# A hybrid decoder layer on one core: the input projection by Strassen's seven products

## What is computed

```
h = rms_norm(x, norm_pre) * (1 + scale(c)) + shift(c)       # scale, shift, gate = silu(c) @ ada_w + ada_b
u = h @ w_in                                                # 1024 x 3720
q, k, v, f_logit, z_rwkv, p_pool, g = split(u)              # 512, 512, 512, 8, 896, 256, 1024 columns
y = concat[forgetting attention(rms_norm(q), rms_norm(k), v, f_logit),
           RWKV-7(z_rwkv), multi-window pooling(p_pool)] * silu(g)
x + gate(c) * rms_norm(y @ w_out, norm_post)
```

## Time and profile before

| | us |
|---|---|
| median of three runs (3635.56 to 3656.0) | 3651.18 |
| span of the profiled execution | 3646.8 |
| prepare, up to the projection's first instruction | 99.7 |
| projection, main part (first f matmul to last g matmul) | 112.5 to 1434.0 |
| recurrence, attention, output | 1439 to 3647 |

### The profile page before, as it was taken

One profiled execution on the slowest core, in us unless ns is written; L12 is line 12 of the kernel. 1 busy time (PEld: TensorE's weight loads), 2 busy tenths in 40 slices (PEclk: granted clock), 3 DMA queues, 4 the chain that ended last, 5 costly groups with the idle time before them and its releaser, 6 DMA issues. The chain is left out here.

```text
span 3646.8 us, 79839 instructions
## 1 busy us (share of the span) xinstructions
PE 3460.6 (95%) x26405; PEld 2109.1 (58%) x26405; DVE 2248.2 (62%) x3692; ACT 1867.6 (51%) x3525; POOL 1613.4 (44%) x2028
## 2 busy tenths in 40 slices
PE   8999999999999997699999599999999999979998
PEld 8444444444444443588888366666666666645444
DVE  7614152433424242688775499889988989964554
ACT  3322232232223233577775477777777777753333
POOL 0113030202112031245553389988889889962222
PEclk9999999999999998699988699999999999989999
DMA  8111212111111112222221221120220211214555
GB/s 331 53 50 67 71 48 65 54 62 54 66 53 65 58 64 77 54 76 81 65 55 36 57 57 34 31 58 9 55 58 8 57 28 36 57 69 161 187 189 182
DMA packets 211044, 267.83 MB, mean 73 GB/s; under 512 B 117309, under 2 KB 163092, under 8 KB 204212
## 3 DMA queue, kind: packets, MB, share of 16 engines
q1 hardware_dynamic: 210171, 262.65, 23.5%
q0 software_dynamic: 480, 0.14, 0.1%
HBM read 165.83 MB, written 96.89 MB: 72 GB/s over the span
## 5 line engine op out<-in xcount | busy, mean ns | idle before, releaser
L2041 ACT ACTIVATE p<-psc,xb,sc 128x512 f32<-128x512 f32 (+3 forms) x1152 | 848.6, 744 | 313.2 <-PE psc L2132 300.6
L2019 POOL TENSOR_TENSOR plo<-p 128x512 f16<-128x512 f32 (+2 forms) x864 | 907.1, 1079 | 64.0 <-ACT p L2041 62.2
L2188 DVE TENSOR_REDUCE mx<-pm 128x1 f32<-128x512 f32 (+3 forms) x1201 | 729.7, 636 | 96.9 <-PE pm L2063 85.0
L2111 PE MATMUL po<-v,p 128*128 128x129 f16 x4224 | 513.4, 220 | 22.6 <-POOL plo L2019 19.2
L2113 PE MATMUL po<-v,plo 128*128 128x65 f16 x4224 | 483.4, 192 | 0.0
L712 POOL CAST stage<-qn 128x512 f16<-128x512 f32 x64 | 39.1, 611 | 971.1 <-DVE qn L597 971.1
L2111 PEld LDWEIGHTS po<-v,p 128*128 128x128 bf16 x4224 | 388.7, 97 | 124.2 <-POOL plo L2019 29.2
L2063 PE MATMUL pm<-ka,qa 128*128 128x512 f16 (+3 forms) x1201 | 437.5, 368 | 2.7 <-DVE mx L2188 2.6
L2113 PEld LDWEIGHTS po<-v,plo 128*128 128x128 f16 x4224 | 379.2, 98 | 96.1
L2130 PE MATMUL psc<-qa,ka 128*128 128x512 f16 (+3 forms) x1152 | 419.2, 364 | 0.0
L2132 PE MATMUL psc<-qb,kb 128*128 128x512 f16 (+3 forms) x1152 | 417.8, 363 | 0.0
(11 more groups left out here) (350 smaller groups left out, 5943.9 us busy)
## 6 DMA issues: line engine op xcount, KB each, us to landing
xt<-in_x SPq DMA_DIRECT2D x36, 512.0 KB, 6.0
scratch_z<-stage SPq DMA_DIRECT2D x72, 256.0 KB, 2.0
y<-scratch_y SPq DMA_DIRECT2D x35, 512.0 KB
g<-scratch_g SPq DMA_DIRECT2D x35, 512.0 KB
xr<-in_x SPq DMA_DIRECT2D x34, 512.0 KB, 6.0
scratch_qk<-stage SPq DMA_DIRECT2D x64, 256.0 KB, 2.6
scratch_g<-stage SPq DMA_DIRECT2D x64, 256.0 KB, 2.0
out<-o SPq DMA_DIRECT2D x32, 512.0 KB, 3.0
```

The lines of the kernel that those rows point to most:

```text
L2019: nc.gpsimd.tensor_tensor(plo[:, k % NP, 0:w], p32[:, k % NP, 0:w], hi[:, 0:w], ALU.subtract)\
L2041: nc.scalar.activation(p32[:, k % NP, 0:w], psc[k % 2][:, 0:w], ACT.Exp, bias=xb[:, u, b, x // 4:x // 4 + 1], scale=m.sc[:, 0:1]).then_inc ...
L2111: nc.tensor.matmul(o[:, oc:oc + VW], hi[:, c0:c0 + P], v[:, u, x, 0:VW], start=(x == 0 and t % 2 == 0), stop=False, skip_group_check=True)
L2188: nc.vector.tensor_reduce(mx[:, s, t, q:q + 1], pm[g][:, 0, 0:w], AX.X, ALU.max).then_inc(pm_d.sem, 1)
```

## The change

`w_in`'s columns are taken in 14 **sets** of 256 (q and k: 4, z without tile 6: 4, g: 4, v: 2), tokens in four **super-blocks** of 1,024. A set in a super-block is a product of two 2 x 2 block matrices (tokens 2 x 512, inputs 2 x 512, columns 2 x 128), made with seven block products instead of eight, in the form with four sums of h (S1 to S4) and four of w (T1 to T4). z tile 6 and f are done as before, `single`, at the start of each super-block.

- **Token sums.** A unit is 128 tokens of either half by 128 inputs of either half: four transposes, ScalarE and VectorE make the four blocks (`raw_high`, `raw_low`), GpSimd four sums (`sums`), ScalarE and VectorE the two pieces of seven operands (`high`, `low`; 7 x 128 columns). 16 units a super-block: the first 16 ahead of all products, the others spread over the second half of the super-block before.
- **Weight sums.** No longer is the whole matrix held. A set is loaded raw (1 MB), scaled and summed on GpSimd (`weight_sums`), split by ScalarE and VectorE (`weights_high`, `weights_low`; 28 x 128 columns each). Sets 0 and 1 are made before the products, 2 to 13 during sets 1 to 6 of the first super-block, two per set (counted from 1), at products 0 and 4. Each is stored to DRAM (`scratch_ws`, 1.84 MB); from the third set on, in every super-block, it is loaded again into a ring of two.
- **Products.** Each is 12 matmuls' worth of 512 columns. Four PSUM banks hold sums; ScalarE copies product 0, VectorE adds at 1, 2, 3, 5 and 6, ScalarE copies at 4; this gives the four tiles of a set, in four buffers `c` and four of `stage`. In g and v the stationary operand is 128 tokens, and 128 weight columns stream.
- **Tiles.** What was done out of PSUM is now done out of `c`, one to four products later. The head norm's inverse is exp(-0.5 ln(mean + eps)) on ScalarE, with the table set loaded by hand each time; no reciprocal.
- **No loop.** 396 steps and the tail are written out; every engine's queue order is fixed in them: at step g it does its part for products g, g-1 and so on.
- **prepare** takes only the row maxima of `w_in`; the gate's third of `ada_w` is left out there and summed by VectorE in the last super-block. x of 1,024 tokens is loaded at the start.

```diff
+        A11, A12, A22, S1, S2, S3, S4, A21 = range(8)
+        B11, B21, B22, T1, T2, T3, T4 = range(7)
+        PRODUCTS = ((A11, B11, 0), (S2, T2, 1), (S3, T3, 2), (S1, T1, 3), (A12, B21, 0), (A22, T4, 2), (S4, B22, 3))
+        ARRIVES = {3: (1, 1), 4: (0, 0), 5: (1, 0), 6: (0, 1)}
...
+                def product(sb_, n, i):
+                    ao, bo, b = PRODUCTS[i]
...
+                    elif i == 4:
+                        pe.wait_ge(p1_d, q + 1)
+                    elif i == 5:
+                        pe.wait_ge(u2_d, q + 1)
+                    else:
+                        pe.wait_ge(c_dve, q * 3 + 1)
+                    fresh = i < 4
+                    for k in range(4):
+                        for x, (l, r) in enumerate(((0, 0), (0, 1), (1, 0))):
+                            first, last = k == 0 and x == 0, k == 3 and x == 2
+                            if kind(n)[0] in ("qk", "z"):
+                                t = nc.tensor.matmul(bank[b][:], m.ring[:, slot, l, bo, k, :], hh[:, side, r, ao, k, :],
+                                                     start=fresh and first, stop=last, skip_group_check=True)
+                            else:
+                                for tp in range(4):
+                                    ts = slice(tp * P, (tp + 1) * P)
+                                    t = nc.tensor.matmul(bank[b][:, ts], hh[:, side, l, ao, k, ts], m.ring[:, slot, r, bo, k, :],
+                                                         start=fresh and first and tp == 0, stop=last, skip_group_check=True)
+                    t.then_inc(mm, 1)
...
+                def head_inverse(x):
+
+                    act.wait_ge(ss_d, x + 1)
+                    nc.scalar.preload_act_table_set(EXP_LN)
+                    activate(sq[:, x % 2, :], pss[:], ACT.Ln, bias=m.eps[:, 0:1]).then_inc(ln_d, 1)
+                    act.wait_ge(ln_d, x + 1)
+                    activate(sq[:, x % 2, :], sq[:, x % 2, :], ACT.Exp, scale=-0.5).then_inc(rec_d, 1)
...
+                def arrives(sb_, n, i):
+
+                    half, side = ARRIVES[i]
+                    t = tile(sb_, n, half, side)
+                    if i == 3:
+                        dve.wait_ge(u2_d, set_of(sb_, n) + 1)
+                    dve.wait_ge(mm, ended(sb_, n, i))
+                    wait_c_free(dve, t)
+                    tt(c[:, t % NC, :], bank[2 if i == 5 else 3][:], (u2 if i == 3 else u1)[:], ALU.add).then_inc(c_dve, 1)
...
+                def sums(u):
+
+                    x = h7[:, u % 2, :, :]
+                    pool.wait_ge(raw_a, u + 1)
+                    pool.wait_ge(raw_v, u + 1)
+                    tt(x[:, S1, :], x[:, A21, :], x[:, A22, :], ALU.add).then_inc(s_step, 1)
+                    tt(x[:, S3, :], x[:, A11, :], x[:, A21, :], ALU.subtract).then_inc(s_step, 1)
+                    pool.wait_ge(s_step, 4 * u + 1)
+                    tt(x[:, S2, :], x[:, S1, :], x[:, A11, :], ALU.subtract).then_inc(s_step, 1)
+                    pool.wait_ge(s_step, 4 * u + 3)
+                    tt(x[:, S4, :], x[:, A12, :], x[:, S2, :], ALU.subtract).then_inc(s_step, 1)
...
+                def weight_sums(q):
+
+                    r = wraw[:, q % 2, :, :]
+                    w = 2 * P if q >= 0 else P + FOX_HEADS
...
+                    tt(r[:, :, 0:w], r[:, :, 0:w], m.rinv[:].unsqueeze(2).to_broadcast([P, KT, w]), ALU.mult).then_inc(w_step, 1)
...
+                    pool.wait_ge(w_lo, q + 1)
+                    tt(wt[:, 0, :, :], b12, b11, ALU.subtract).then_inc(w_step, 1)
+                    tt(wt[:, 2, :, :], b22, b12, ALU.subtract).then_inc(w_step, 1)
+                    pool.wait_ge(w_step, done + 2)
+                    tt(wt[:, 1, :, :], b22, wt[:, 0, :, :], ALU.subtract).then_inc(w_step, 1)
+                    pool.wait_ge(w_step, done + 4)
+                    tt(wt[:, 3, :, :], b21, wt[:, 1, :, :], ALU.subtract).then_inc(w_sums, 1)
...
+                weight_sums(-1)
+                for u in range(16):
+                    sums(u)
+                    if u == 8:
+                        weight_sums(0)
+                weight_sums(1)
...
+                for g in range(NG + LAST):
+                    if unit_at(sub(g - 1)) is not None:
+                        sums(unit_at(sub(g - 1)))
+                    if sub(g - 4) is not None:
+                        sb_, n, i = sub(g - 4)
+                        if n and kind(n)[0] == "qk":
+                            for half, side in tails((sb_, n, i)):
+                                pieces(sb_, n, half, side)
+                    if sub(g - 2) is not None and is_pool(sub(g - 2)[1]):
+                        sb_, n, i = sub(g - 2)
+                        for half, side in tails((sb_, n, i)):
+                            trailing(sb_, n, half, side)
+                    if production(sub(g)) is not None:
+                        weight_sums(production(sub(g)))
...
+        m.kinds = (("qk", 0), ("z", 7), ("qk", 1), ("z", 0), ("qk", 2), ("z", 2), ("qk", 3), ("z", 4),
+                   ("g", 0), ("g", 1), ("g", 2), ("g", 3), ("v", 0), ("v", 1))
```

More of the change, by code:

```diff
@@ L357, in project @@
[L357 to L378 removed]
+        hh = m.h
@@ new lines, in sub, with ended, set_of, kind @@
+        def sub(g):
+            if not 0 <= g < NG:
+                return None
+            sb_, r = divmod(g, SUBS)
+            return (sb_, 0, 0) if r == 0 else (sb_, 1 + (r - 1) // NP7, (r - 1) % NP7)
+        def ended(sb_, n, i):
+            return sb_ * SUBS + (0 if n == 0 else 1 + (n - 1) * NP7 + i) + 1
+        def set_of(sb_, n):
+            return sb_ * NSET + n - 1
+        def kind(n):
+            return m.kinds[n - 1]
+        def tile(sb_, n, half, side):
+            if n == 0:
+                return sb_ * TILES + half
+            return sb_ * TILES + 2 + (n - 1) * 4 + {(1, 1): 0, (0, 0): 1, (1, 0): 2, (0, 1): 3}[half, side]
@@ new lines, in tails, with qk_number @@
+        def tails(at):
+            if at is None:
+                return ()
+            n, i = at[1:]
+            if n == 0:
+                return (0, 0), (1, 0)
+            if i not in ARRIVES:
+                return ()
+            if kind(n)[0] == "z":
+                return {3: (), 4: ((0, 0),), 5: ((1, 0),), 6: ((0, 1), (1, 1))}[i]
+            return (ARRIVES[i],)
+        def qk_number(sb_, n, half, side):
+            return (sb_ * 4 + kind(n)[1]) * 4 + {(1, 1): 0, (0, 0): 1, (1, 0): 2, (0, 1): 3}[half, side]
@@ new lines, in _ @@
+                sp.dma_start(fbc[:], a.fox_f_bias[0:1, :].partition_broadcast(P)).then_inc(fb_in, 16)
+                load_raw(1)
+                keep(0)
+                load_raw(2)
+                keep(1)
+                for g in range(NG + LAST):
+                    at = sub(g)
+                    for half, side in tails(sub(g - 6)):
+                        store(*sub(g - 6)[0:2], half, side)
+                    if at is not None:
+                        sb_, n, i = at
+                        q = production(at)
+                        if q is not None and q + 1 < NSET:
+                            load_raw(q + 1)
+                        if n >= 1 and i == 0 and 2 <= set_of(sb_, n) + 1 < NSB * NSET:
+                            load_ring(set_of(sb_, n) + 1)
+                    q = production(sub(g - 3))
+                    if q is not None:
+                        keep(q)
+                    if group_at(sub(g + 4)) is not None:
+                        load_x(sub(g + 4)[0] + 1, group_at(sub(g + 4)))
+                    if at is not None and at[0] == NSB - 1 and at[1] <= KT and at[2] == 2:
+                        if at[1] >= 1:
+                            load_gate(at[1] - 1)
@@ new lines, in head_means @@
+                def head_means(x):
+                    pe.wait_ge(sq_d, x + 1)
+                    if x:
+                        pe.wait_ge(ln_d, x)
+                    nc.tensor.matmul(pss[:], m.headmean[:], sq[:, x % 2, :], start=True, stop=True).then_inc(ss_d, 1)
+                for u in range(16):
+                    turn(u)
+                for g in range(NG + LAST):
+                    at = sub(g)
+                    if at is not None:
+                        if at[1] == 0:
+                            single(at[0])
+                        else:
+                            product(*at)
+                    if unit_at(at) is not None:
+                        turn(unit_at(at))
+                    if sub(g - 2) is not None:
+                        sb_, n, i = sub(g - 2)
+                        if n and kind(n)[0] == "qk":
+                            for half, side in tails((sb_, n, i)):
+                                head_means(qk_number(sb_, n, half, side))
@@ new lines, in low, with x_scaled @@
+                def low(u):
+                    side, j, k = u // 16 % 2, u // 4 % 4, u % 4
+                    js = slice(j * P, (j + 1) * P)
+                    dve.wait_ge(hi_made, u + 1)
```

(27 more changed lines are left out.)

987 lines of the change are left out of this document (586 added, 401 removed).

## The result

The changed kernel takes 3758.33 us (median of 4 runs, 3741.48 to 3761.63) against 3653.49: ratio 1.0293, 95% interval 1.0259 to 1.0327. I had forecast 3641 with a range of 3568 to 3718, so a slightly faster kernel; it is slower and lies outside the range.

The account below looks back on a forecast made before the run. TensorE's own pace was taken to bound the projection. Its new end, 155.5 + (1155 - 14) + 71 + 43 + 10 + 3 = 1423.5 against 1434.0 us, gave -10.5 us and so 3641 us, range 3568 to 3718.

Parts of the forecast that it names:

- TensorE's work: Projection's matmuls: 1155 us after the change, a gain of 164 on 1319, with 128-column matmuls at 0.055 us.
- rival 3: Projection: 128-column matmuls take 0.081 us each, adding 230 us, so the kernel takes 3871 us; chance 0.03.
- Preparation: Stage before the projection: loads become the pace and the projection starts at 82.5 us, 17 us earlier.
- The fill: Units and first weights made before set 1: 73 us, bounds 60 and 90, so set 1 starts at 155.5.
- meetings in the fill and the weights: Before set 1: 3 us for two-input operations of GpSimd and VectorE that meet.
- Production: Making twelve weight sets in the first super-block: 71 us with the pooled tiles' part there, 54 like for like without it.
- the series through `wt`: Weight production: GpSimd's sums 4.9, ScalarE's high 3.2 and VectorE's low 3.9 in turn through one buffer, 12.0 us each.
- set 3 as the longest: First super-block: set 3 takes some 43 us, held by the pooled tiles' trailing work; sets 1, 2, 4, 5, 6 take 24 to 27.
- Pooled tiles: Super-blocks 1 to 3: GpSimd's trailing work holds set 3's first tile, 14.4 x 3 = 43 us, bounds 20 and 65.
- Elsewhere the slack holds: Other projection work, such as ln, exp and table load (2.7 us in steps of 3.45), costs TensorE nothing.
- Rival 2: GpSimd and VectorE, both with two SBUF inputs, slow each other 1.5 times: +93 us, 3734 us; chance 0.18.
- Later stages: Stages after the projection read the same layouts, so their time changes by nothing.

Follow-up runs that it names:

- everything on VectorE: Changed kernel with token sums and whole weight sums, multiplication included, made by VectorE, GpSimd keeping pieces and pooled tiles; 3725.2 us, ratio 1.0200.
- short trailing: Changed kernel with the pooled tiles' trailing sums on GpSimd done for the first 32 tokens of a tile instead of 512; 3708.9 us, ratio 1.0171.

## Why the prediction was wrong, step by step

- **TensorE's work, held.** The g and v sets take 18.76 us for 336 matmuls, 55.8 ns each against my 55; rival 3 is refuted, and with it, for this kernel, the 81 ns of the Trainium skill ("TensorE: Matmul & The Clock Gate", Back-to-back issue gap).
- **Preparation, nearly.** The projection begins at 85.3 us, 82.5 forecast.
- **The fill: 73 forecast, 93 taken.** Undisturbed units come 2.8 to 3.7 us apart, mean 3.3, not 2.6. The meetings with GpSimd are the cause: with the low parts as copies the units come 2.6 to 2.7 apart, as forecast, and the fill is 7 us shorter, where I had 3 for meetings in the fill and the weights. (ScalarE's and VectorE's raw halves run one after the other, where I had counted one; by the same rows that costs at most 0.1 us a unit.) GpSimd's first sums came 7 us late by the gap of the stage's start. The same gap, 8.05 us, stands before GpSimd's index instruction in the trace of before, where nothing waited for it; I didn't ask who now would. No run takes it away alone, so its 7 us are read from the timeline and not tested, and some 8 of the 20 stay without a cause that a run shows.
- **Production: 54 forecast, 90 taken.** That production is what makes super-block 0 long is shown: without it the 90 us are gone. Two things in my step failed. The term of 12.0 us for the series through `wt` is 15.0; of those 3 us VectorE's low part has 2.1: 0.6 from interpolating between two sizes, 1.5 from the lock. And the series is not all that paces production: weight sets come 19.3 us apart, and 16 apart where the series is some 8. I had set 3 as the longest with 43; set 2 takes 51, with the stop of 17.24 us in it, and set 3 takes 37. How the 36 us divide between the term and the queues stays open. (A slip of words: the 19.8 us that I gave a set in the forecast hold two head means of 0.86, not four; it is the mean of a q or k set and a z set.)
- **Pooled tiles: 43 forecast, 41.8 taken** in super-blocks 1 to 3, by the mechanism forecast: GpSimd begins 16 us into set 2 and takes 27.5 (17 and 27.6 forecast). Shortened in super-block 0 they give 9, not 17.
- **"Elsewhere the slack holds": 0 forecast, 44 taken.** The largest wrong step by size. It added the new operations and compared them with a step, without the square that shares their queue, the wait in front of that, and the single bank behind which the next mean stands. The run with one load in 16 tiles shows it.
- **Rival 2, half right.** Its mechanism is there, its form wrong. It cost 7 us in the fill and, with all of GpSimd's part cut, at most 34 in production; the trailing work of super-blocks 1 to 3, which the rival raised by 14 us each, took what it would alone, 27.5 us.
- **Later stages: 0 forecast, 18.5 in the profile.** The code is the same, and over the 13 profiles of the table the rest varies from 2224 to 2259 us, which is 2202 to 2237 from the recurrence's start (22 us behind the last copy), where before had 2207.6. It goes with the clock granted in the recurrence: from 390 to 790 us behind the last copy it was 0.82 with everything on VectorE (rest 2259), 0.83 in the changed kernel (2248), 0.88 with short trailing (2224). Why it is granted differently from run to run I did not find, nor whether a part of the 18.5 belongs to the change.

By size, set 1 late by 23 (preparation's 3 and the fill's 20), production 36 and table loads 44 are the 103 us by which the recurrence started late against the forecast. Where they arise is shown by the runs; inside the fill and production the division is in part argued.

## What to carry over

A faster algorithm on the busiest engine is paid for on the others: price the added work as a chain through its one buffer, with everything that stands ahead of it in each in-order queue (the chain was busy 15 us a weight set, and took 19.3), and hold that, not busy time, against the slack. Where GpSimd and VectorE both run on SBUF, a meeting costs the whole remaining instruction of the first (up to 3.4 us behind GpSimd's multiplication, up to 0.9 behind VectorE's subtraction of 896 columns), so a long instruction on either is the greater danger. And an idle gap in the old profile is free only until something new is queued behind it.

## What the runs showed of the chip

- GpSimd and VectorE with two SBUF inputs exclude each other: 8 columns on GpSimd 0.20 us alone, 1.08 behind a VectorE subtraction; VectorE's 896 columns 1.09 alone, 3.48 behind a GpSimd multiplication of 3.60; a contiguous one-input copy 0.41 to 3.82; a one-input copy of 896 columns (1.09) leaves GpSimd's 0.46 as it is.
- GpSimd idles about 7 us after its first instructions of the projection, with either of two instructions next (6.89 and 7.35; 8.05 in the kernel before).
- Streaming 128 columns with a weight load each keeps 55.8 ns a matmul over sets of 336.
- A table load is 1.28 us each time, also where the set it asks for was the last one loaded.
